# A two-block network on one NeuronCore: the boundaries between its stages, multiplied in two halves of the tokens

## What is computed

```python
h = h + 0.5 * rmsnorm(swiglu(rmsnorm(h, ffn1_pre), gate, up, down), ffn1_post)      # stage A
u = rmsnorm(h, mix_pre)                                                             # stage B
y1 = ssd_branch(u @ w_in ...); y2 = diff_attn_branch(u @ w_in ...)
h = h + rmsnorm((g1 * y1 + g2 * y2) @ w_out, mix_post)
h = h + 0.5 * rmsnorm(swiglu(rmsnorm(h, ffn2_pre), ...), ffn2_post)                 # stage C
# the second block takes 0.5 * h of w_out into h, and so on
u = rmsnorm(h, norm1)                                                               # stage D
h = h + (g1 * gated_delta_rule(...) + g2 * sparse_attention(...)) @ w_out_2
up = dwconv(rmsnorm(h, norm2) @ w_up) + b                                           # stage E
h = h + (silu(up_gate) * up_value) @ w_down
return rmsnorm(h, final_g)
```

## Time and profile before

| | us |
|---|---|
| median of 3 runs | 2860.5 (2860.01 to 2862.3) |
| the profiled execution | 2860.19 |
| its span in the profile | 2858.4 |
| PE busy | 2618.0 (92%) |
| DVE busy | 1500.9 (53%) |
| ACT busy | 1125.3 (39%) |
| POOL busy | 125.9 (4%) |

### The profile page before, as it was taken

How to read it: one execution, slowest core, us unless ns; L and a number is a source line. 1 busy time by engine, 2 the same in 40 slices (tenths; PEclk the granted TensorE clock), 3 DMA queues, 4 the chain that set the end, 5 groups by cost and what they waited for, 6 DMA issues and landing times. The chain is left out here.

```text
span 2858.4 us, 33690 instructions
## 1 busy us (share of the span) xinstructions
PE 2618.0 (92%) x13778; PEld 2044.9 (72%) x13778; DVE 1500.9 (53%) x2280; ACT 1125.3 (39%) x1687; POOL 125.9 (4%) x98
## 2 busy tenths in 40 slices
PE   8999978998998999988999978988898997899998
PEld 6888846766776776767888846756667675688886
DVE  5444266656566664345443254587644445466632
ACT  4222234555544455443222234242424255344422
POOL 0000020000000000010000020000000000100000
PEclk9999989999999999999999988999999998999999
DMA  4333312221221221222233311111111110233332
GB/s 139 97 102 91 101 52 69 67 68 58 82 72 47 74 67 59 82 81 74 96 96 98 94 54 59 53 52 38 52 38 45 60 59 23 74 96 96 98 99 76
DMA packets 59193, 209.93 MB, mean 73 GB/s; under 512 B 6560, under 2 KB 6560, under 8 KB 59040
## 3 DMA queue, kind: packets, MB, share of 16 engines
q1 hardware_dynamic: 57600, 204.38, 22.8%
q10 hardware_dynamic: 1440, 3.41, 0.3%
HBM read 205.66 MB, written 2.10 MB: 73 GB/s over the span
## 5 line engine op out<-in xcount | busy, mean ns | idle before, releaser
L1349 PE MATMUL bank<-uR,hl 128*128 128x512 f32 x2232 | 923.2, 414 | 54.5 <-DVE uR L1962 27.1
L1350 PE MATMUL bank<-uR,hl 128*128 128x512 f32 x2232 | 885.6, 397 | 0.0
L1351 PE MATMUL bank<-uR,hl 128*128 128x512 f32 x2232 | 884.5, 396 | 0.0
L1950 DVE TENSOR_TENSOR hl<-raw,hl 128x1024 fp32r<-128x1024 f32 (+1 forms) x391 | 473.1, 1210 | 618.1 <-ACT hl L1668 617.3
L1349 PEld LDWEIGHTS bank<-uR,hl 128*128 128x128 f32 x2232 | 429.0, 192 | 189.9 <-issue 67.5
L1668 ACT CAST hl<-raw 128x1024 fp32r<-128x1024 f32 (+1 forms) x391 | 402.4, 1029 | 249.4 <-PE bank L1351 248.3
L1351 PEld LDWEIGHTS bank<-uR,hl 128*128 128x128 f32 x2232 | 428.2, 192 | 93.7
L1350 PEld LDWEIGHTS bank<-uR,hl 128*128 128x128 f32 x2232 | 429.2, 192 | 85.9 <-issue 5.2
L1349 PE MATMUL bank<-act,hl 128*128 128x512 f32 x528 | 205.4, 389 | 0.0
L1350 PE MATMUL bank<-act,hl 128*128 128x512 f32 x528 | 205.4, 389 | 0.0
L1351 PE MATMUL bank<-act,hl 128*128 128x512 f32 x528 | 205.4, 389 | 0.0
(11 more groups left out here) (434 smaller groups left out, 2595.3 us busy)
## 6 DMA issues: line engine op xcount, KB each, us to landing
raw<-in_win SPq DMA_DIRECT2D x147, 512.0 KB, 3.5
raw<-in_w SPq DMA_DIRECT2D x44, 512.0 KB, 3.5
raw<-in_w1g SPq DMA_DIRECT2D x22, 512.0 KB, 3.5
raw<-in_w1u SPq DMA_DIRECT2D x22, 512.0 KB, 3.5
raw<-in_w2g SPq DMA_DIRECT2D x22, 512.0 KB, 3.5
raw<-in_w2u SPq DMA_DIRECT2D x22, 512.0 KB, 3.5
raw<-in_w1d SPq DMA_DIRECT2D x16, 512.0 KB, 3.5
raw<-in_wssd SPq DMA_DIRECT2D x16, 512.0 KB, 3.6
```

Source lines behind the costliest of these rows:

```text
L1349: e.matmul(s.bank[:, :], h[:, 0, w], hi, start=s.first and q == 0, stop=False)
L1350: e.matmul(s.bank[:, :], h[:, 0, w], lo, start=False, stop=False)
L1351: i = e.matmul(s.bank[:, :], h[:, 1, w], hi, start=False, stop=s.last and q == n - 1)
L1950: e.tensor_tensor(h[:, 1, 0:s.width], x[:, 0:s.width], h[:, 0, 0:s.width].bitcast(F), ALU.subtract).then_inc(*sig("dve_split.lo", s))
```

## The change

Tokens are cut in two halves, columns 0 to 255 and 256 to 511. At each boundary the last output blocks are multiplied for the first half alone, and then for the second half; the norms run once for each half; and the first three panels of the next stage (`lead`) are multiplied for the first half and then for the second. `seam` writes this order: `first` (first halves of the last blocks), `second` (their second halves), then the leads; what is hung in `between` follows the named step. A panel whose second half is still to come keeps its `hl` buffer (`keep`, `done_with`), and splits are put into the list only when their buffer is free. In a down projection three buffers hold the three panels of m = 7 alone, so those of m = 6 are loaded and split a second time. In stages B and D three panels are kept (m = 5, 6, 7). The leads' banks are filled in advance, and `ugemm` takes them with no panel of its own. The fold is parted in `fold_u`, which writes `uR`, and `fold_squares`, which takes the squares of the full width after the leads. The lines of the engines' programs get `s.at` as their columns; line numbers move by about 130 (1349 to 1351 become 1475 to 1477, 1668 is 1795, 1950 is 2077).

```diff
+FULL = slice(0, L)
+HV = (slice(0, L // 2), slice(L // 2, L))
...
+    phase, widths, held = {"split": 0}, {}, set()
+
+    def next_splits():
+
+        while phase["split"] < stream["n"] + NHL - 1 and phase["split"] - NHL not in held:
+            j = phase["split"]
+            splits[j] = step("split", j=j, width=widths.get(j, 0))
+            phase["split"] += 1
...
+    def panel(src, width, keep=False):
         j = stream["n"]
         stream["n"] += 1
         step("load", j=j, src=src, width=width)
-        splits[j]["width"] = width
-        splits[j + NHL - 1] = step("split", j=j + NHL - 1, width=0)
+        widths[j] = width
+        if j in splits:
+            splits[j]["width"] = width
+        if keep:
+            held.add(j)
+        next_splits()
         return j
 
-    def mm(j, bank, xs, first, last, off=0):
-        s = step("mm", j=j, bank=bank, xs=xs, first=first, last=last, off=off)
+    def done_with(j):
+        held.remove(j)
+        next_splits()
+
+    def mm(j, bank, xs, first, last, off=0, at=FULL):
...
+        if ahead:
+            b = ahead.pop(0)
...
+    def fold_u(gname, last, hv=None):
+        at = FULL if hv is None else HV[hv]
+        s = step("fold_u", g=gname, h=[t[0] + t[1] if hv is None else list(t[hv]) for t in t_h], last=last, at=at)
+        for k in range(KB):
+            for i in (0, 1) if hv is None else (hv,):
+                t_u[k][i] = [("dve_norm.lo", s, k)]
...
+    def fold_squares():
         acc = fp.take()
         qs = []
-        s = step("fold", g=gname, h=[list(t) for t in t_h], last=list(u_last), qs=qs)
+        s = step("fold_sq", h=[t[0] + t[1] for t in t_h], qs=qs)
...
+    def norm(gname, hv, last, r, xs):
+        s, b = sumsq(hv, xs)
+        s2 = step("norm", g=gname, h=[list(t[hv]) for t in t_h], last=last, s=s, b=b, r=r, xs=xs, at=HV[hv])
         b.release(("act_norm.ln", s2))
...
+    def post(P, hv, half, r):
+        r = rstd([(P.acc[:, HV[hv]], P.ct[hv])], O1024, HV[hv], r)
+        s = step("post", ys=[P.y[k] for k in range(KB)], yt=[P.t[k][hv] for k in range(KB)], r=r, half=half,
+                 h=[list(t[hv]) for t in t_h], hr=[list(t) for t in t_hr], at=HV[hv])
         for k in range(KB):
-            t_h[k] = [("dve_post.h", s, k)]
-        for k in (0, 2, 1, 4, 3, 6, 5, 7):
-            ys[k].release(*t_h[k])
-        r.release(*t_h[KB - 1])
-
-    def down(src, a, ta):
-        for m in range(KB):
+            t_h[k][hv] = [("dve_post.h", s, k)]
...
+    def lead(i, src, hv):
+
+        if hv == 0:
+            ahead.append(MB.take())
+            ahead[i].j = panel(src, KB * 128, True)
+        for _ in u_steps(ahead[i].j, ahead[i], hv):
+            pass
+        if hv == 1:
+            done_with(ahead[i].j)
+
+    def seam(first, second, between, srcs):
+
+
+        for f in first:
+            f()
+        for i, f in enumerate(second):
+            f()
+            between.get(("second", i), lambda: None)()
+        for i, src in enumerate(srcs):
+            lead(i, src, 0)
+            between.get(("lead", i), lambda: None)()
+        for i, src in enumerate(srcs):
+            lead(i, src, 1)
...
+    DOWN = ((0, 8), (8, 8), (16, 6))
+
+    def down(src, a, ta, done):
+        def part(m, b, at, n, hv=None, j=None):
+            if j is None:
+                j = panel(src[m, :, at * 128:(at + n) * 128], n * 128, m == KB - 1)
+            b.t = [mm(j, b, [(a[:, 0, k, :], a[:, 1, k, :], ta[k]) for k in range(at, at + n)], at == 0, at + n == FB, 0,
+                      FULL if hv is None else HV[hv])]
+            return j
...
+        for m in range(KB - 2):
             b = MB.take()
-            at = 0
-            for n in (8, 8, 6):
-                j = panel(src[m, :, at * 128:(at + n) * 128], n * 128)
+        bs, js = {}, []
+
+        def whole(m):
+            bs[m] = MB.take()
+            js[:] = [part(m, bs[m], at, n, 0) for at, n in DOWN]
+            done(m, bs[m], 0, m == KB - 1)
+
+        def piece(m, i, again):
+            at, n = DOWN[i]
+            if i == 0:
+                bs[m] = SB.take()
+            part(m, bs[m], at, n, 1, None if again else js[i])
+            if not again:
+                done_with(js[i])
+            if i == 2:
+                done(m, bs[m], 1, again)
+
+        return ([lambda m=m: whole(m) for m in (KB - 2, KB - 1)],
+                [lambda m=m, i=i: piece(m, i, m == KB - 2) for m in (KB - 1, KB - 2) for i in range(3)], bs)
+
+    def outward(src, P8, done):
+
+        def part(m, b, hv=None, j=None):
+            if j is None:
+                j = panel(src[m], KB * 128, m >= KB - 3)
+            b.t = [mm(j, b, P8, True, True, 0, FULL if hv is None else HV[hv])]
+            return j
+
+        for m in range(KB - 3):
+            b = MB.take()
+            part(m, b)
+            done(m, b)
+        bs, js = {}, {}
+
+        def begin(m):
+            bs[m] = MB.take()
+            js[m] = part(m, bs[m], 0)
+            done(m, bs[m], 0, m == KB - 1)
+
+        def end(m):
+            bs[m] = SB.take()
+            part(m, bs[m], 1, js[m])
+            done_with(js[m])
+            done(m, bs[m], 1, m == KB - 1)
+
+        return [lambda m=m: begin(m) for m in range(KB - 3, KB)], [lambda m=m: end(m) for m in range(KB - 3, KB)], bs
+
...
+        seam(first, second, {("second", 0): lambda: posted(0), ("second", 3): lambda: normed(0),
+                             ("lead", 0): lambda: posted(1), ("lead", 2): lambda: normed(1)}, srcs)
...
+        fold_u("ffn2_pre", last, hv)
+
+    seam(first, second, {("second", 0): lambda: posted(0), ("lead", 0): lambda: posted(1)},
+         (d["w2g"][0], d["w2u"][0], d["w2g"][1]))
...
+    seam(first, second, {("second", 0): lambda: norm("norm2", 0, last, r, xs), ("lead", 0): lambda: norm("norm2", 1, last, r, xs)},
+         (W3[0], W3[FB], W3[1]))
...
+    def finish(hv):
+        s, b = sumsq(hv, xs)
+        return step("final", s=s, b=b, r=r, h=[list(t[hv]) for t in t_h], at=HV[hv])
+
+    ends_at = []
+    seam(first, second, {("second", 0): lambda: ends_at.append(finish(0))}, ())
+    step("store", s=ends_at[0], at=HV[0])
+    step("store", s=finish(1), at=HV[1])
...
-                e.matmul(s.bank[:, :], h[:, 0, w], hi, start=s.first and q == 0, stop=False)
-                e.matmul(s.bank[:, :], h[:, 0, w], lo, start=False, stop=False)
-                i = e.matmul(s.bank[:, :], h[:, 1, w], hi, start=False, stop=s.last and q == n - 1)
+                e.matmul(s.bank[:, s.at], h[:, 0, w], hi[:, s.at], start=s.first and q == 0, stop=False)
+                e.matmul(s.bank[:, s.at], h[:, 0, w], lo[:, s.at], start=False, stop=False)
+                i = e.matmul(s.bank[:, s.at], h[:, 1, w], hi[:, s.at], start=False, stop=s.last and q == n - 1)
...
```

More of the change, by code:

```diff
@@ L267, in build @@
     s_init = step("init")
-    t_h = [[(f"x{k}_in", None, 16)] for k in range(KB)]
+    t_h = [[[(f"x{k}_in", None, 16)], []] for k in range(KB)]
     t_hr = [[] for _ in range(KB)]
-    t_u = [[] for _ in range(KB)]
+    t_u = [[[], []] for _ in range(KB)]
     u_last = []
+    ahead = []
     late = {}
@@ L274, in build @@
     splits, ends = {}, {}
-    phase = {"c": 0}
-    for j in range(NHL - 1):
-        splits[j] = step("split", j=j, width=0)
+    phase, widths, held = {"split": 0}, {}, set()
[5 more added lines that the diff above has]
+    next_splits()
     step("setup", s=s_init)
-    def panel(src, width):
+    def panel(src, width, keep=False):
         j = stream["n"]
@@ L1292, in build @@
         p.release(*ta[j])
[L1293 to L1306 removed]
+    first, second, bs = down(d["w3d"], act[2], ta, lambda m, b, hv=None, end=False: add_h(m, b, 1.0, hv))
+    xs, r = [fp.take() for _ in range(KB)], fp.take()
+    def finish(hv):
[5 more added lines that the diff above has]
+    step("store", s=finish(1), at=HV[1])
     def sync_program(e):
```

301 lines of the change are left out of this document (148 added, 153 removed).

## The result

The changed kernel takes 2890.3 us (median of 4 runs, 2890.07 to 2892.31), the kernel before 2861.1: ratio 1.0103, 95% interval 1.0086 to 1.0121. It is slower by 29 us where 18.5 us less were forecast. The profiled execution has a span of 2888.2 us against 2858.4, 29.8 more. PE is busy 2653.0 us (2618.0 before), the mean granted clock 0.957 (0.962).

The account below looks back on a forecast made before the run. PE was busy 92%; its 80.9 us idle in five boundary stretches bounded the gain. Gains 4.5 + 3.7 + 7.7 + 5.5 less 2.9 give 18.5 off 2860.2: 2842 us, range 2815 to 2862.

Parts of the forecast that it names:

- The list of side work in stages B and D: Stages B and D: small steps shift by nine places; priced at 0, within 5 us either way.
- sign of being wrong: Half products over 0.128 us apart, no PE waits at the named places, or long stretches changing by over 5 us.
- Half products: All 1656 half products: starts 0.117 us apart, costing 6.3 us in all over exactly half.
- third rival: All 1656 half products: weight loads not hidden, at 0.192 each 2966 us; chance of slower than 2866, 0.12.
- two rules weighed in the prediction: Weight loads on PE: overlap only to other row groups, or load into a background buffer; the second was taken.
- Boundary A: First boundary, stretch of 80.8 us: gain of 10.5 less 5 for dt's chain and 1 for clock, 4.5 us.
- list of signs: Products 0.117 apart, named PE waits in boundaries A and B, five stretches at about 74, 54, 71, 46 and 47.
- Boundary C: Built like A, from 79.3 to 69.1 us, less 1 for the bank and 1.5 for clock: gain 7.7 us.
- Boundary B: Stretch of 57.9 us: 5.7 less 2 for clock, gain 3.7 us; squares behind splits, PE waits for scale.
- Boundary D: Stretch of 51.2 us becomes 45.7, with 2.5 of clock for two 4 us idles: gain 5.5 us.
- The end: Last stretch, 44.3 us becomes 47.2 with half-width blocks and norm: loss 2.9 us.
- Waits take the place of waits: Second rival, four boundaries: dearer half-width operations and clock drops lose 14 us, 2856; chance of 2855 to 2866, 0.10.

Follow-up runs that it names:

- before_places: The kernel before, with the first three panels of stages B and D no longer giving way to small steps (nine places missing in each): 2885.3 us, ratio 1.0079.
- slots: The changed kernel, with each lead taken in the stage using up four places of the list instead of one: 2876.1 us, ratio 1.0044.
- lazyB: The changed kernel, with the leads' second halves multiplied where the leads are taken, in boundary B only: 2889.8 us, ratio 1.0096.
- best_sum: lazy_con_end, with boundary B's sum of squares standing on PE behind the second half of lead 1 instead of lead 0: 2847.3 us, ratio 0.9949.
- lazy_con_end: lazy, with the constants' load moved back between the second post and second norm, and the last stage's end of full width: 2850.2 us, ratio 0.9951.
- endfull: The changed kernel, with the last stage's output blocks and last norm of full width again: 2889.2 us, ratio 1.0097.
- lazy: The changed kernel, with the leads' second halves multiplied where the leads are taken, in every boundary with leads: 2856.7 us, ratio 0.9984.
- con: The changed kernel, with the load of the stage's constants moved back between the second post and the second norm: 2889.2 us, ratio 1.0091.

## Why the prediction was wrong, point by point

**The step that failed** is the last of the sum: "The list of side work in stages B and D shifts by the nine places at which the leads no longer give way; their PE waits are many and small, and I put that at 0, within 5 either way." before_places measured it by itself: some 23 us (24.6 in its trace), about half of the 48 us between forecast and result. The prediction's own sign of being wrong, a long stretch that changes by more than 5 us, came true with 21.3. The shift was seen in the order and given no price. Nor are the waits small: in stage B of the kernel before 13 waits of over 1.5 us make 47 of the 58 us of idle, and some are followed by work at the lower level. What moves them costs on both counts, 8.7 us of idle and about 8 us of slower panel products in the first 190 us of the stage.

**The other half** is in the boundaries and their sum. Against before_places, which has the same places missing, the changed kernel is 5 us slower where 18.5 less were forecast. By the table: A 0.2 (forecast -4.5), B 2.4 (-3.7), C -2.5 (-7.7), D -1.4 (-5.5), the end 4.3 (2.9), the start 1.6 and stage D 0.3 (none). This takes the two halves as a sum. slots shows that they are not quite one: with the places back, the changed kernel regains 14 us and not 23; a wait of 11.36 us for the scan stands there now.

**Half products.** Forecast 0.117 apart, measured 0.120: 1656 x 0.003 = 5 us more than the 6.3. The pair of fp32 products gave the right size. The third rival fell. Of the two rules weighed in the prediction the trace agrees with that of Part 2 of "TensorE: Matmul & The Clock Gate" (Trainium skill), a load into the background: 0.19 of load and 256 columns fit into 0.12, and every load takes all rows.

**Boundary A.** Its gain was forecast at 4.5 and is 2.1 to the 73rd product (81.5 became 79.4). The 74 in the prediction's list of signs doesn't fit its own sum, as 80.8 less 4.5 is 76.3. The small operations were sized rightly: `post` of a half takes 8.0 and 7.6 us on DVE (forecast 8.0), `norm` 6.2 (6.5). Lead 0 was forecast to wait for its split until 41.8 and waited until 44.1; the leads were to end at 69.1 and end at 75.0. The first half's sum was put at one wait of 5.7; measured are three of 0.5 to 1.3, as POOL's pairs come one by one. The restart at the lower clock was booked with 1 us; 48 of the half products go at the lower level here, 0.09 us more each, 4.3 us. Then the wait for dt's bank is 4.24 (forecast 1.5) and the one for the scan 2.34 (2.5 to 4.5). Not seen was the constants' load, a DMA that the change moved behind two waiting splits (issue 381.07 to 420.50); DVE waits 2.07 for it, and some of what lies between it and dt is late too.

**Boundary C.** 79.3 became 77.0, forecast 71. It pays a bank wait of 1.96 at its end. The restarts at the lower clock were booked with 1.5; 57 of its half products go at the lower level (57 x 0.09 = 5.1 us).

**Boundary B.** The mechanism was right (squares behind the splits, waits for the sum and for `scale`), the size not: the stretch is 56.6, forecast 54, with the wait of 2.31 for `scale` in it, and the products at the lower level behind that wait add 2.2 in the next. Gain -0.8 instead of 3.7. lazyB takes the queued squares out and best_sum moves the sum; on top of the other changes of lazy_con_end they reach 9.1.

**Boundary D.** Forecast 46, measured 49.8. The wait ahead of the sum is 3.19 (forecast over 4), but the sum itself takes 3.75 us of PE (2491.52), where I had put 0.6. Its eight matmul records (two for each of the four products) follow without a wait between them, 0.43 us apart, at the lower level.

**The end.** Forecast a loss of 2.9, measured 4.3, by the forecast mechanism; endfull gives it back whole.

**The start.** 1.7 us that no step has: behind the first sum PE came back at the lower clock in this execution (below). It is the execution and not the order.

**The rivals.** "Waits take the place of waits" was nearest in mechanism, at 2856. It takes 14 us from the boundaries; 23 are missing there by the sum above. Its cause was only in part the right one: the operations of half width cost what was forecast (boundary A above), and more of the half products than were booked go at the lower level. It has nothing for the stages behind.

Not settled: which single small step of stage B sets off the wait of 5.7 us, and how the 21 us of the stage divide between waits and clock if only one of them is changed. The runs moved blocks of places, not one step.

## What to carry to other kernels

Where one list orders all engines, a change that takes out points at which side work gets its turn moves all interleaved work behind them. Price that move first, best by making it alone in the old kernel; here it cost more than the edit was worth. Follow each DMA issue and each wait that the new order puts ahead of it, not only the arithmetic. Splitting a dependency into halves pays where the engines' queues are in the order in which the halves get ready: the same halves gave +29 us with the leads' second halves in a block and -5 with each where its lead is used (lazy), which also gives the small steps their places back.

## What the hardware showed that was not expected

The clock after a short wait differs between executions of one order. At the first sum of the program, which starts at nearly the same time in both kernels (21.76 and 21.90), PE waited 1.91 us in the kernel before and went on at full level; in the changed one it waited 2.26 and went on at the lower:

```profile
21.76 1.10 PE L1366 MATMUL bank<-fA,onesc 128*128 128x512 f32 x2 [1.91 <-DVE fA L1969]
...
23.15 0.39 PE L1351 MATMUL bank<-uR,hl 128*128 128x512 f32 x1
```

```profile
21.90 1.10 PE L1493 MATMUL bank<-fA,onesc 128*128 128x512 f32 x2 [2.26 <-DVE fA L2099]
...
23.50 0.63 PE L1477 MATMUL bank<-uR,hl 128*128 128x512 f32 x1
```

It costs 1.7 us, and con, with the same order there, waited 1.56 and didn't pay it. In the 17 traces of this case the wait at this place was 1.41 to 2.12 us in the eleven that went on at full level and 2.14 to 2.72 in the six that went on at the lower. The program has many waits of 2 to 4 us. That they fall now on one side and now on the other would explain the 3 to 4 us by which equal stretches differ; it was not tested.
